# A two-layer encoder on one core: other loads ahead of the weights, x turned through two pairs of banks, and short chains moved between stages

## The chip, the cores and the metric

The kernel runs on one core of a Trainium2 chip. The metric is the device time in microseconds (us), the median of three runs. Lower is better.

## What is computed

Two pre-norm layers over x of 512 tokens by 1024 features, all in float32, with weights read from device memory once. Cut to what matters:

```
# layer 0
h = rmsnorm(x, mix_norm[0]);  proj = h @ w_in             # 1024 x 5376
a_q, a_k = axial_rope(rmsnorm(a_q, q_norm)), axial_rope(rmsnorm(a_k, k_norm))   # 8 / 2 heads of 64
a_o = softmax(a_q * scale @ a_k) @ a_v                    # dense
b_o = mix of three banded attentions (window, dilation) = (128,1), (512,4), (2048,16)
x = x + [a_o, b_o] @ w_out;  x = x + swiglu(rmsnorm(x, ffn_norm[0]))
# layer 1
proj = rmsnorm(x, mix_norm[1]) @ w_in;  u = conv4(proj right) + conv_b
r, i = sigmoid(gate_a(u)), sigmoid(gate_x(u));  log_a = -8 * r * softplus(-lam)
x = x + ((scan forward + scan backward) * gelu(proj left)) @ w_out
x = x + swiglu(rmsnorm(x, ffn_norm[1]));  final rmsnorm
```

## The kernel before, in words

Every product of a weight matrix is made of three TensorE products, high x high, high x low and low x high, written by `mm3` (L1330 to L1332). Activations stand feature by token (`h_hi`, `h_lo`), 8 tiles of 128 features. The weights come in chunks through a ring of four buffers (`RING`). SP loads a chunk into `w_stage` (L360) once the chunk four before it is split (`chunk_lo`). ScalarE copies the high part to `w_hi` (L505) once TensorE has used the chunk four before (`chunk_used`). GpSimd subtracts and writes `w_lo` (L453), and TensorE multiplies. Each engine has its order written out by hand, and semaphores tie them together, so an instruction that waits holds all that is written behind it on its engine.

The order of the stages on TensorE: a prologue; 16 chunks of the first projection (two for each of eight k, 18 products a k); four pairs p = 0 to 3 with 24 chunks each (numbered j = 0 to 23, about nine products each), between whose chunks the attention is woven in; the output projection; the first FFN; the odd layer; the second FFN.

**The prologue.** SP loads x in four parts of 128 tokens (`x_tok`, L371), then the first weight chunks. ScalarE issues 13 small loads (`head_sel`, L556; eight vectors into `p_rows`, L562; the q and k gains into `qk_rows`, L565), then loads its table for the square root (L573) and squares the four parts of x (L578). TensorE turns each part of x (`x_turn`, L1349, eight transposes) into PSUM banks 6 and 7, and VectorE copies them to `x_t` (L863); a turn waits for the copy of the one before. Between turns 1 and 2 TensorE turns the parameter rows (L1365, L1366), once all 13 loads are in. `idle_products` (L1341) are products of zeros whose result nobody reads. After the last copy come the root means: `diag`, a product that spreads them (L1355), `rstd_a`, and h, which is x times gain times root mean.

**The first pair (p = 0).** `first_pair(j)` on TensorE, ScalarE and VectorE holds what turns the first projection into q and k of the dense attention: gains, squares (`sq_qk`), sums of squares by head (L1402, 20 small products, 40 in the trace, with 2 columns each), roots, `k_rb` (L1408), `ak`. The scores of the four blocks (L1430) stand at j = 10, 13, 16 and 19, and the turning of their probabilities (L1442) at j = 13, 16, 19 and 22. VectorE makes the maxima (`a_stat`, L1019), and after ScalarE's exponential (L662) scales the probabilities (`prob_a`, L1027). At j = 11 VectorE also works through `softplus_out` (L925 to L939), 16 instructions of 128x16 that are needed first in the odd layer.

In the first FFN VectorE ends the norm with `rstd_wide` (L968); then come the gate products of a group (L1167), four chunks ahead of which ScalarE and GpSimd must have the next weights split.

## Time and profile before

| | us |
|---|---|
| median of three runs (1390.64 to 1395.12) | 1392.08 |
| the profiled execution, its time | 1390.08 |
| its span | 1388.3 |
| TensorE busy | 1310.5 (94%) |
| GpSimd, VectorE, ScalarE busy | 646.1, 554.7, 549.5 |

The page follows one execution. TensorE is busy for 94% of the span, each other engine for less than half. The chain of work that ended last, by engine: TensorE 51%, issue 21%, GpSimd 11%, VectorE 11%. A view in order of time gives for each merged group its start, its length, the engine, line, operation and operands, and in brackets the idle time before it with what ended it.

### The profile page before, as it was taken

The numbers are of one execution on the slowest core, as the hardware profiler recorded it, in microseconds if no ns is written. First come the engines' busy times: TensorE is split into PE (matmuls) and PEld (weight loads), VectorE is DVE, ScalarE is ACT, GpSimd is POOL, SyncE is SP. The second block draws the span as 40 slices with busy tenths as digits, with TensorE's granted clock in tenths as the row PEclk, the third lists the DMA queues.
The fourth block names the chain that finished last, engine by engine and source line by source line (L and its number), as shares of the span: only waits on it lengthen the run. The fifth ranks groups of instructions, "written<-read, shape, count | busy, mean of one in ns | idle before, by whom it ended". The sixth has DMA issues, their size and how long they took to land.

```text
span 1388.3 us, 18821 instructions
## 1 busy us (share of the span) xinstructions
PE 1310.5 (94%) x6606; PEld 1056.2 (76%) x6606; DVE 554.7 (40%) x881; ACT 549.5 (40%) x999; POOL 646.1 (47%) x512
## 2 busy tenths in 40 slices
PE   7998999999999999999999987957899999999996
PEld 5876787777778888888888876746688888888885
DVE  4358575665644312212102146978652221210102
ACT  3434444444444333333323327558343332332322
POOL 2556464555535444454444443524544444444440
PEclk9999999999999999999999998979899999999997
DMA  4622212222313333333222241213233333332221
GB/s 141 199 57 60 62 55 65 58 66 64 122 52 114 95 96 97 98 97 96 96 97 98 76 148 64 84 47 121 70 105 99 97 92 98 97 100 97 92 91 60
DMA packets 118725, 125.74 MB, mean 91 GB/s; under 512 B 7945, under 2 KB 98313, under 8 KB 118025
## 3 DMA queue, kind: packets, MB, share of 16 engines
q1 hardware_dynamic: 118272, 124.88, 29.0%
q8 instruction: 37, 0.61, 0.2%
q14 instruction: 24, 0.19, 0.0%
q10 hardware_dynamic: 392, 0.07, 0.0%
HBM read 118.62 MB, written 6.29 MB: 90 GB/s over the span
## 4 chain that ended last, share of the span: by engine, by line
PE 51%; issue 21%; POOL 11%; DVE 11%; ACT 4%; DMA 2%; ACTq 0%; POOLq 0%; DVEq 0%; SPq 0%
PE ps L1330 15%; PE ps L1331 14%; PE ps L1332 14%; POOL w_lo L453 10%; DVE r_g L1283 2%; DVE i_g L1278 1%; PE ps L1453 1%; DVE u_f L1214 1%; PE ps L1488 1%; PE ps L1465 1%; PE ps L1430 1%; PE ps L1469 1%; POOL rot L462 1%; DMA w_stage<-in_odd_w_in_dram 1%; DVE a_g L1293 1%
## 5 line engine op out<-in xcount | busy, mean ns | idle before, releaser
L453 POOL TENSOR_TENSOR w_lo<-w_stage,w_hi 128x512 fp32r<-128x512 f32 (+2 forms) x456 | 581.0, 1280 | 711.9 <-ACT w_hi L505 711.7
L505 ACT ACTIVATE w_hi<-w_stage 128x512 fp32r<-128x512 f32 (+2 forms) x456 | 268.8, 595 | 636.9 <-PE ps L1332 622.5
L1330 PE MATMUL ps<-h_hi,w_hi 128*128 128x512 f32 x1104 | 439.6, 398 | 6.3 <-POOL w_lo L453 3.2
L1331 PE MATMUL ps<-h_lo,w_hi 128*128 128x512 f32 x1104 | 431.9, 391 | 0.0
L1332 PE MATMUL ps<-h_hi,w_lo 128*128 128x512 f32 x1104 | 431.7, 391 | 0.0
L1330 PEld LDWEIGHTS ps<-h_hi,w_hi 128*128 128x128 f32 x1104 | 208.8, 189 | 68.0 <-issue 16.5
L1332 PEld LDWEIGHTS ps<-h_hi,w_lo 128*128 128x128 f32 x1104 | 208.4, 189 | 44.1
L1331 PEld LDWEIGHTS ps<-h_lo,w_hi 128*128 128x128 f32 x1104 | 208.9, 189 | 41.9 <-issue 1.0
L1167 DVE TENSOR_TENSOR silu_g<-ps,rstd_wide 128x512 f32<-128x512 f32 x44 | 30.2, 686 | 331.7 <-PE ps L1332 331.7
L1330 PE MATMUL ps<-f_hi,w_hi 128*128 (+1 forms) x352 | 137.0, 389 | 0.0
L1332 PE MATMUL ps<-f_hi,w_lo 128*128 (+1 forms) x352 | 136.9, 389 | 0.0
L1331 PE MATMUL ps<-f_lo,w_hi 128*128 (+1 forms) x352 | 136.9, 389 | 0.0
L1140 DVE TENSOR_TENSOR x_t<-x_t,ps 128x512 f32<-128x512 f32 x32 | 21.0, 681 | 234.6 <-PE ps L1332 234.6
L1330 PEld LDWEIGHTS ps<-f_hi,w_hi 128*128 128x128 f32 x352 | 66.1, 188 | 13.8
L1332 PEld LDWEIGHTS ps<-f_hi,w_lo 128*128 128x128 f32 x352 | 66.1, 188 | 13.7
L1331 PEld LDWEIGHTS ps<-f_lo,w_hi 128*128 128x128 f32 x352 | 66.1, 188 | 13.6
L662 ACT ACTIVATE prob_a<-ps,a_stat,exp_scale 128x512 f32<-128x512 f32 x32 | 24.6, 774 | 52.9 <-DVE a_stat L1020 52.9
L1330 PE MATMUL ps<-s_hi,w_hi 128*128 128x512 f32 x64 | 27.3, 426 | 11.8 <-DVE s_lo L1301 6.0
L1330 PE MATMUL ps<-u_hi,w_hi 128*128 128x512 f32 x32 | 15.7, 492 | 23.5 <-DVE u_raw L1229 16.0
L1332 PE MATMUL ps<-w_hi,h_lo 128*128 128x256 f32 x128 | 36.1, 282 | 0.0
L1330 PE MATMUL ps<-w_hi,h_hi 128*128 128x256 f32 x128 | 36.1, 282 | 0.0
L1331 PE MATMUL ps<-w_lo,h_hi 128*128 128x256 f32 x128 | 36.1, 282 | 0.0
(205 smaller groups left out, 1460.4 us busy)
## 6 DMA issues: line engine op xcount, KB each, us to landing
w_stage<-in_ffn_w_gate_up_dram SPq DMA_DIRECT2D x176, 256.0 KB, 3.1
w_stage<-in_ffn_w_down_dram SPq DMA_DIRECT2D x88, 256.0 KB, 2.7
w_stage<-in_even_w_in_dram SPq DMA_DIRECT2D x96, 192.0 KB, 2.5
w_stage<-in_odd_w_in_dram SPq DMA_DIRECT2D x32, 256.0 KB, 2.5
x_spill<-x_t SPq DMA_DIRECT2D x2, 2048.0 KB, 8.1
x_t<-x_spill SPq DMA_DIRECT2D x2, 2048.0 KB, 7.7
w_stage<-in_odd_w_out_dram SPq DMA_DIRECT2D x16, 256.0 KB, 2.8
w_stage<-in_even_w_out_dram SPq DMA_DIRECT2D x16, 192.0 KB, 2.4
```

Of the source, the lines that this page charges most:

```text
L453: pool.tensor_tensor(out=w_lo[:, s, 0:n], in0=stage[:, s, 0:n], in1=w_hi[:, s, 0:n].bitcast(f32), op=ALU.subtract).then_inc(chunk_lo, 1)
L462: pool.tensor_tensor(out=rot[:, g, :], in0=q_f[:, g, :], in1=tab(K_SINB, T), op=ALU.mult).then_inc(sin_done, 1)
L505: act.activation(w_hi[:, j % RING, 0:n], stage[:, j % RING, 0:n], ACT.Copy).then_inc(chunk_hi, 1)
L662: act.activation(prob_a[:, hh, :], ps[:, hh, :], ACT.Exp, scale=exp_scale[:, p, c, hh:hh + 1], bias=a_stat[:, 1, hh:hh + 1], accum_out=a_s ...
L1140: V.tensor_tensor(x_t[:, j, :], x_t[:, j, :], ps[:, b0 + m, :], ALU.add).then_inc(x_new, 1)
L1167: V.tensor_tensor(silu_g[:, q, :], ps[:, b0 + q, :], rstd_wide[:, :], ALU.mult).then_inc(gate_scaled, 1)
L1214: ins = V.scalar_tensor_tensor(out=u_f[:, n, :], in0=u_raw[:, n % 4, w:w + T], scalar=tap, in1=u_f[:, n, :], op0=ALU.mult, op1=ALU.add)
L1278: driven[t] = step.mark(V.tensor_tensor(i_g[:, t, :], i_g[:, t, :], m_g[:, t, :], ALU.mult))
L1283: scanned[u] = step.mark(V.tensor_tensor_scan(out=r_g[:, u, way], data0=a_g[:, u, way], data1=i_g[:, u, way], initial=0.0, op0=ALU.mult, o ...
L1330: pe.matmul(out_, lh, rh, start=start, stop=False, skip_group_check=skip)
L1331: pe.matmul(out_, lh, rl, start=False, stop=False, skip_group_check=skip)
L1332: return pe.matmul(out_, ll, rh, start=False, stop=stop, skip_group_check=skip)
```

## The change

It does five things.

1. ScalarE issues one load (`mix_norm`, into `mix_rows`) in place of 13. The other 12 are issued by SP, behind the load of weight chunk 4. Those rows are turned on TensorE after k = 5 of the first projection, and copied by VectorE at the end of its first-norm work; the first pair waits for them (`params_ready`).
2. x is turned through banks 6, 7 and 2, 3 by turns, so that a turn waits for the copy of the turn before the last. Fewer idle products stand between.
3. The sums of squares of q and k stand at j = 2, 3, 4 and 5 (4, 4, 8, 4 products) in place of all 20 at j = 4. The turning of v goes from j = 3 to 5, the root from 5 to 6, `k_rb` from 7 to 8, `ak` from 8, 9 to 9, 11.
4. VectorE's `aq_rope(0)` goes from j = 6 to j = 4.
5. `softplus_out` goes from j = 11 of the first pair to the first FFN, behind `rstd_wide`.

```diff
@@ -373,6 +374,17 @@
                 k = c // 2
                 col, n = (512, 256) if c % 2 else (0, 512)
                 load(c, c, stage[:, c % RING, 0:n], w_even[rows(k), col:col + n])
+                if c == 4:
+                    sync.dma_start(head_sel[:, :], A["consts"][:, K_HEAD:K_HEAD + 2]).then_inc(params_in, 16)
+                    for at_, name, n in ((G_FFN, "ffn_norm", 16), (G_FINAL, "final_norm", 8),
+                                         (CONV_W, "odd_conv_w", 32), (CONV_B, "odd_conv_b", 8), (GA_B, "odd_gate_a_b", 16),
+                                         (GX_B, "odd_gate_x_b", 16), (LAM, "odd_lambda", 16)):
+                        v = A[name]
+                        flat = {1: "(n p) -> n p", 2: "l (n p) -> (l n) p", 3: "a l (n p) -> (a l n) p"}[len(v.shape)]
+                        sync.dma_start(p_rows[at_:at_ + n, :], v.rearrange(flat, p=P)).then_inc(params_in, 16)
+                    for n, name in enumerate(("even_q_norm", "even_k_norm")):
+                        for half in range(2):
+                            sync.dma_start(qk_rows[n:n + 1, half * HD:(half + 1) * HD], A[name]).then_inc(params_in, 16)
...
@@ -444,6 +456,7 @@
             pool.memset(ones[:, :], 1.0).then_inc(ones_set, 1)
+            pool.memset(p_rows[0:G_FFN, :], 0.0).then_inc(ones_set, 1)
             pool.memset(bkf[:, :], 0.0).then_inc(pads_zeroed, 1)
@@ -553,16 +566,7 @@
-            act.dma_start(head_sel[:, :], A["consts"][:, K_HEAD:K_HEAD + 2]).then_inc(params_in, 16)
-            for at_, name, n in ((G_MIX, "mix_norm", 16), (G_FFN, "ffn_norm", 16), (G_FINAL, "final_norm", 8),
-                                 (CONV_W, "odd_conv_w", 32), (CONV_B, "odd_conv_b", 8), (GA_B, "odd_gate_a_b", 16),
-                                 (GX_B, "odd_gate_x_b", 16), (LAM, "odd_lambda", 16)):
-                v = A[name]
-                flat = {1: "(n p) -> n p", 2: "l (n p) -> (l n) p", 3: "a l (n p) -> (a l n) p"}[len(v.shape)]
-                act.dma_start(p_rows[at_:at_ + n, :], v.rearrange(flat, p=P)).then_inc(params_in, 16)
...
+            act.dma_start(mix_rows[0:G_FFN, :], A["mix_norm"].rearrange("l (n p) -> (l n) p", p=P)).then_inc(mix_in, 16)
 
             def first_root(c0, c1):
 
@@ -608,18 +613,18 @@
                     for m in (2 * j - 2, 2 * j - 1):
                         act.wait_ge(aq_scaled, m + 1)
                         act.activation(sq_qk[:, m, :], ps[:, m, :], ACT.Square).then_inc(sq_done, 1)
-                if j == 4:
+                if j == 5:
                     act.wait_ge(v_a_turned, 1)
                     act.activation(av[:, :, :].rearrange("p c d -> p (c d)"), ps[:, 2, :], ACT.Copy).then_inc(av_in, 1)
-                if j == 5:
+                if j == 6:
                     act.wait_ge(qk_ms, 1)
                     act.activation(rstd_qk[:, :, :, :], rstd_qk[:, :, :, :], ACT.Sqrt).then_inc(qk_sqrt, 1)
                     act.activation(scratch[:, :], ones[:, 0:1], ACT.Exp)
-                if j == 6:
+                if j == 7:
                     act.wait_ge(lam_exp_in, 1)
                     act.activation(sp[:, 1, :], sp[:, 1, :], ACT.Exp, scale=-1.0).then_inc(lam_exp, 1)
-                if j in (8, 9):
-                    m = j - 8
+                if j in (9, 11):
+                    m = (j - 9) // 2
                     act.wait_ge(k_roped, 1)
                     for half in (m, 1 - m):
                 dve.wait_ge(x_turned, c + 1)
-                V.tensor_copy(x_t[:, :, c * P:(c + 1) * P], ps[:, 6:8, :].rearrange("p b (j t) -> p (b j) t", t=P)).then_inc(x_raw, 1)
+                b0 = 2 if c % 2 else 6
+                V.tensor_copy(x_t[:, :, c * P:(c + 1) * P], ps[:, b0:b0 + 2, :].rearrange("p b (j t) -> p (b j) t", t=P)).then_inc(x_raw, 1)
 
             def first_ms_part(c0, c1):
@@ -890,9 +896,8 @@
-            dve.wait_ge(params_turned, 1)
-            step.mark(V.tensor_copy(params[:, :], ps[:, 1, 0:P]))
-            V.tensor_copy(qk_gain[:, :], ps[:, 1, P:P + 2]).then_inc(params_ready, 1)
+            dve.wait_ge(mix_turned, 1)
+            mix_copied = step.mark(V.tensor_copy(params[:, 0:G_FFN], ps[:, 1, 0:G_FFN]))
             x_in_place(2)
             first_ms_part(0, 3)
@@ -911,6 +916,9 @@
                 h_scaled(k)
             h_lo_part(KD - 2)
             h_lo_part(KD - 1)
+            dve.wait_ge(params_turned, 1)
+            step.mark(V.tensor_copy(params[:, G_FFN:P], ps[:, 6, G_FFN:P]))
+            V.tensor_copy(qk_gain[:, :], ps[:, 6, P:P + 2]).then_inc(params_ready, 1)
 
             def softplus_in():
                     dve.wait_ge(chunk_used, C_PAIR)
@@ -993,10 +1002,13 @@
                 if j == 4:
+                    dve.wait_ge(aq_scaled, 4)
+                    aq_rope(0)
+                if j == 5:
                     dve.wait_ge(ssq_ready, 1)
                     flat = rstd_qk[:, :, :, :].rearrange("p t c h -> p (t c h)")
                     V.tensor_scalar(flat, ps[:, 4, 0:40], 1.0 / HD, EPS, ALU.mult, ALU.add).then_inc(qk_ms, 1)
-                if j == 5:
+                if j == 6:
                     dve.wait_ge(qk_sqrt, 1)
                     flat = rstd_qk[:, :, :, :].rearrange("p t c h -> p (t c h)")
                     step.done(V.reciprocal(flat, flat))
@@ -1004,14 +1016,9 @@
-                if j == 6:
-                    dve.wait_ge(aq_scaled, 4)
-                    aq_rope(0)
-                if j == 7:
+                if j == 8:
                     dve.wait_ge(k_rb, 1)
                     V.tensor_tensor(k_f[:, :], k_f[:, :], ps[:, 3, :], ALU.mult).then_inc(k_roped, 1)
-                if j == 11:
-                    softplus_out()
 
             def a_step(p, c):
@@ -1156,6 +1163,8 @@
 
             def ffn(n, nn, next_gain, fb):
                 late_rms(nn, 4 - fb)
+                if n == 0:
+                    softplus_out()
@@ -1343,10 +1352,11 @@
             def x_turn(c):
 
                 pe.wait_ge(x_in[c], 16)
-                if c:
-                    pe.wait_ge(x_raw, c)
+                if c >= 2:
+                    pe.wait_ge(x_raw, c - 1)
+                b0 = 2 if c % 2 else 6
                 for j in range(KD):
-                    last = pe.transpose(ps[:, 6 + j // 4, (j % 4) * P:(j % 4 + 1) * P], x_tok[:, c, j * P:(j + 1) * P], ident[:, :])
+                    last = pe.transpose(ps[:, b0 + j // 4, (j % 4) * P:(j % 4 + 1) * P], x_tok[:, c, j * P:(j + 1) * P], ident[:, :])
                 last.then_inc(x_turned, 1)
@@ -1359,21 +1369,20 @@
             idle_products(6)
             pe.wait_ge(consts_in, 16)
             x_turn(0)
+            idle_products(2)
+            x_turn(1)
+            pe.wait_ge(mix_in, 16)
+            pe.transpose(ps[:, 1, 0:G_FFN], mix_rows[0:G_FFN, :], ident[0:G_FFN, 0:G_FFN]).then_inc(mix_turned, 1)
+            idle_products(2)
+            x_turn(2)
+            idle_products(2)
+            x_turn(3)
             idle_products(3)
-            x_turn(1)
-            pe.wait_ge(params_in, 16 * 13)
-            pe.transpose(ps[:, 1, 0:P], p_rows[:, :], ident[:, :])
-            pe.transpose(ps[:, 1, P:P + 2], qk_rows[0:2, :], ident[0:2, 0:2]).then_inc(params_turned, 1)
+            pe.wait_ge(ones_set, 2)
+            first_spread(0, 3)
             idle_products(3)
-            x_turn(2)
-            idle_products(4)
-            x_turn(3)
-            idle_products(2)
-            pe.wait_ge(ones_set, 1)
-            first_spread(0, 3)
-            idle_products(4)
             first_spread(3, 4)
-            idle_products(8)
+            idle_products(6)
 
             for k in range(KD):
@@ -1384,24 +1393,29 @@
+                if k == 5:
+                    pe.wait_ge(params_in, 16 * 12)
+                    pe.transpose(ps[:, 6, 0:P], p_rows[:, :], ident[:, :])
+                    pe.transpose(ps[:, 6, P:P + 2], qk_rows[0:2, :], ident[0:2, 0:2]).then_inc(params_turned, 1)
 
 
             def first_pair(j):
 
-                if j == 3:
+                if j in (2, 3, 4, 5):
+                    for t in {2: (4,), 3: (0,), 4: (1, 2), 5: (3,)}[j]:
+                        pe.wait_ge(sq_done, 1 if t == 4 else t + 2)
+                        for c in range(NC):
+                            at_ = 2 * (NC * t + c)
+                            last = pe.matmul(ps[:, 4, at_:at_ + 2], sq_qk[:, t, c * P:(c + 1) * P], head_sel[:, :], start=True, stop=True)
+                    if j == 5:
+                        last.then_inc(ssq_ready, 1)
+                if j == 5:
                     pe.wait_ge(v_f_in, 1)
-                    pe.wait_ge(sq_done, 5)
                     pe.wait_ge(aq_scaled, 4)
                     for c in range(NC):
                         last = pe.transpose(ps[:, 2, c * P:(c + 1) * P], v_f[:, c * P:(c + 1) * P], ident[:, :])
                     last.then_inc(v_a_turned, 1)
-                if j == 4:
-                    for t in range(5):
-                        for c in range(NC):
-                            at_ = 2 * (NC * t + c)
-                            last = pe.matmul(ps[:, 4, at_:at_ + 2], sq_qk[:, t, c * P:(c + 1) * P], head_sel[:, :], start=True, stop=True)
-                    last.then_inc(ssq_ready, 1)
-                if j == 7:
+                if j == 8:
                     pe.wait_ge(half_ones_set, 3)
                     pe.wait_ge(k_diag, 2)
@@ -1542,6 +1556,8 @@
                     attention(p, j)
                     c = C_PAIR + p * PAIR_CHUNKS + j
                     part, k = divmod(j, KD)
+                    if p == 0 and j == 0:
+                        pe.wait_ge(params_ready, 1)
                     chunk_ready(c)
                     s = c % RING
                     if part < 2:
```

On TensorE in the prologue the program has these rows. `zeros` are the idle products, `ident,x_tok` a turn of x, `diag,ones` the spreading of the root means. Before:

```order
L1341 MATMUL ps<-zeros 128x512 x6
L1349 MATMUL ps<-ident,x_tok 128x128 x8
L1341 MATMUL ps<-zeros 128x512 x3
L1349 MATMUL ps<-ident,x_tok 128x128 x8
L1365 MATMUL ps<-ident,p_rows 128x128
L1366 MATMUL ps<-ident,qk_rows 128x2
L1341 MATMUL ps<-zeros 128x512 x3
L1349 MATMUL ps<-ident,x_tok 128x128 x8
L1341 MATMUL ps<-zeros 128x512 x4
L1349 MATMUL ps<-ident,x_tok 128x128 x8
L1341 MATMUL ps<-zeros 128x512 x2
L1355 MATMUL ps<-diag,ones 128x384
```

The same place after the change:

```order
L1350 MATMUL ps<-zeros 128x512 x6
L1359 MATMUL ps<-ident,x_tok 128x128 x8
L1350 MATMUL ps<-zeros 128x512 x2
L1359 MATMUL ps<-ident,x_tok 128x128 x8
L1375 MATMUL ps<-ident,mix_rows 128x16
L1350 MATMUL ps<-zeros 128x512 x2
L1359 MATMUL ps<-ident,x_tok 128x128 x8
L1350 MATMUL ps<-zeros 128x512 x2
L1359 MATMUL ps<-ident,x_tok 128x128 x8
L1350 MATMUL ps<-zeros 128x512 x3
L1365 MATMUL ps<-diag,ones 128x384
```

Behind turn 1 stands one turn of `mix_rows` where the two turns of all parameters stood.

On VectorE at j = 10 to 13 of the first pair, before (`a_stat` and `prob_a` belong to the dense attention, `softplus_work` to the odd layer, `rot` and `bq` to the rotary part of the banded one):

```order
L1025 RECIPROCAL a_stat<-a_stat 128x2
L1027 TENSOR_SCALAR prob_a<-prob_a,a_stat 128x512 x2
L925 TENSOR_SCALAR softplus_work<-softplus_work 128x16
L926 RECIPROCAL softplus_work<-softplus_work 128x16
L927 TENSOR_TENSOR softplus_work<-softplus_work 128x16
...
L939 TENSOR_SCALAR decay_neg<-softplus_work 128x16
L1055 STREAM_SHUFFLE rot<-rot 128x512
L1066 TENSOR_TENSOR bq<-q_f,rot 128x4x4x32
L1078 COPY pta<-ps 128x4x128
L1019 TENSOR_REDUCE a_stat<-ps 128x2
```

And after:

```order
L1032 RECIPROCAL a_stat<-a_stat 128x2
L1034 TENSOR_SCALAR prob_a<-prob_a,a_stat 128x512 x2
L1062 STREAM_SHUFFLE rot<-rot 128x512
L1073 TENSOR_TENSOR bq<-q_f,rot 128x4x4x32
L1085 COPY pta<-ps 128x4x128
L1026 TENSOR_REDUCE a_stat<-ps 128x2
```

The softplus rows are gone from between `prob_a` and the next maximum; they now stand between `rstd_wide` and the first gate product of the first FFN.

## Rows read from the trace of the kernel before

**Rows 1.** Timeline of PE, prologue: start us, us, engine, line, op, operands, [idle<-releaser]

```profile
6.11 1.06 PE L1349 MATMUL ps<-ident,x_tok 128*128 128x128 f32 x8 [1.86 <-DMA x_tok<-in_x_dram]
...
11.61 0.38 PE L1365 MATMUL ps<-ident,p_rows 128*128 128x128 f32 x1 [1.97 <-DMA qk_rows<-in_even_k_norm_dram]
...
13.56 1.82 PE L1349 MATMUL ps<-ident,x_tok 128*128 128x128 f32 x8
...
26.18 0.50 PE L1330 MATMUL ps<-h_hi,w_hi 128*128 128x512 f32 x1 [0.71 <-DVE h_lo L889]
```

**Rows 2.** Timeline of DVE, prologue

```profile
7.21 1.23 DVE L863 COPY x_t<-ps 128x1024 f32<-128x1024 f32 x1 [5.80 <-PE ps L1349]
...
17.90 1.22 DVE L863 COPY x_t<-ps 128x1024 f32<-128x1024 f32 x1 [1.18 <-PE ps L1349]
```

**Rows 3.** Timeline of ACT, prologue

```profile
7.11 1.28 ACT L573 ACT_TABLE_LOAD   x1 [7.11 <-issue]
```

**Rows 4.** The tile `x_tok`: time from issue to landing of its four loads

```profile
DMA to landing us min/median/max: 4.8/6.1/7.7
```

**Rows 5.** Timeline of SP, the loads of x and of chunks 4 and 5

```profile
1.20 1.85 SPq L371 DMA_DIRECT2D x_tok<-in_x_dram  x4
...
19.89 2.16 SPq L360 DMA_DIRECT2D w_stage<-in_even_w_in_dram  x2
```

**Rows 6.** DMA issues of the first 60 us: count, KB each, median us to landing

```profile
w_stage<-in_even_w_in_dram SPq DMA_DIRECT2D x8, 256.0 KB, 2.8
```

**Rows 7.** Windows: us, PE, PEld, DVE, ACT, POOL busy (count), granted clock, DMA, GB/s

```profile
19.00:20.00 1.00, 0.00 (x0) 0.00 (x0) 0.97 (x3) 0.00 (x0) 0.86 (x1) 1.00 0.00 0
...
73.00:75.00 2.00, 2.00 (x7) 1.57 (x6) 0.00 (x0) 0.00 (x0) 0.00 (x0) 0.55 0.00 0
75.00:77.00 2.00, 2.00 (x7) 1.54 (x7) 0.06 (x1) 0.72 (x3) 0.14 (x1) 0.60 0.00 0
...
110.00:115.00 5.00, 4.56 (x16) 2.38 (x17) 4.96 (x6) 2.45 (x5) 4.96 (x4) 0.66 0.36 103
```

**Rows 8.** Timeline of PE, first pair, from the sums of squares to j = 19

```profile
68.16 4.52 PE L1402 MATMUL ps<-head_sel,sq_qk 128*128 128x2 f32 x40
...
80.37 1.88 PE L1408 MATMUL ps<-diag,half_ones 128*128 128x512 f32 x4
...
85.59 0.47 PE L1330 MATMUL ps<-h_hi,w_hi 128*128 128x512 f32 x1 [1.25 <-ACT q_f L634]
...
97.20 1.03 PE L1442 MATMUL ps<-ident,prob_a 128*128 128x128 f32 x8
...
110.02 0.63 PE L1442 MATMUL ps<-ident,prob_a 128*128 128x128 f32 x4 [4.38 <-DVE prob_a L1027]
...
120.69 0.63 PE L1442 MATMUL ps<-ident,prob_a 128*128 128x128 f32 x4
```

**Rows 9.** Timeline of PE, second pair, j = 13 and j = 19

```profile
181.08 1.03 PE L1442 MATMUL ps<-ident,prob_a 128*128 128x128 f32 x8
...
197.94 0.63 PE L1442 MATMUL ps<-ident,prob_a 128*128 128x128 f32 x4
```

**Rows 10.** Timeline of DVE, first pair, j = 11

```profile
96.55 1.26 DVE L925 TENSOR_SCALAR softplus_work<-softplus_work 128x16 f32<-128x16 f32 x1
...
103.51 0.17 DVE L935 TENSOR_SCALAR softplus_work<-softplus_work 128x16 f32<-128x16 f32 x1
...
104.14 0.17 DVE L939 TENSOR_SCALAR decay_neg<-softplus_work 128x16 f32<-128x16 f32 x1
```

**Rows 11.** Timeline of DVE, then of ACT, start of the first FFN

```profile
451.43 0.69 DVE L968 COPY rstd_wide<-ps 128x512 f32<-128x512 f32 x1 [4.02 <-PE ps L1595]
454.27 0.69 DVE L1167 TENSOR_TENSOR silu_g<-ps,rstd_wide 128x512 f32<-128x512 f32 x1 [2.15 <-PE ps L1332]
...
458.73 0.61 ACT L505 ACTIVATE w_hi<-w_stage 128x512 fp32r<-128x512 f32 x1
```

**Rows 12.** Timeline of POOL, first pair, j = 11

```profile
96.31 1.47 POOL L468 TENSOR_TENSOR q_f<-q_f,table 128x512 f32<-128x512 f32 x1
```

12 lines of the change are left out of this document (6 added, 6 removed).

## The prediction, made before the changed kernel ran
> **What bounds the kernel now.** I read the shares of busy time first: TensorE works 94% of the span, so what counts is where it waits and where its clock is low. The list of its waits and the windows with the granted clock then show three places that this change touches. (1) The prologue. The first product of the first projection starts at 26.18 us [rows 1]. TensorE had turned parts 0 and 1 of x by 9.64 us, then sat 1.97 us until the last of ScalarE's 13 small loads was in, at 11.61, and turn 2, at 13.56, took 1.82 us for what turn 0 did in 1.06 [rows 1]. The copy of part 3 starts on VectorE at 17.90 [rows 2], and from there a chain of copies, root means and h runs to 26.18. (2) The middle of the first pair. Forty products of two columns keep TensorE busy for 4.52 us [rows 8]; just behind them the clock is 0.55 and 0.60 for 4 us, half speed (1.2 in place of 2.4 GHz) for most of it [rows 7]. A wait of 1.25 us for ScalarE's `q_f` follows at j = 8 [rows 8]. (3) The turn at j = 16, which waits 4.38 us for `prob_a` [rows 8], with the clock at 0.66 over the 5 us from 110 [rows 7]. VectorE was at `softplus_out` from 96.55 to 104.31 us, 7.8 us in all [rows 10], and its next maximum stands behind that. From the projection at 26.18 up to the sums TensorE has no gap to speak of: 8 x 18 + 4 x 9 = 180 products from 26.18 to 68.16, less some 0.6 us for turning v, is 0.23 us each; so a k takes 4.1 us and a chunk of the pair 2.1.
>
> **The prologue.** With one load on its queue instead of 13, ScalarE's table load (at 7.11 [rows 3]) and its squares no longer come behind the issues; the squares then follow the landing of x. The loads of x land 4.8 to 7.7 us after issue [rows 4]; the last of the four goes out at about 2.6 [rows 5], so it is in by 10.3. Turn 0 is bound by its load, as before: 6.11 to 7.17, copy 7.21 to 8.44 [rows 1, 2]. Turn 1 goes to the other banks: two idle products (0.5, estimated from 0.23 each) put it at 7.7 to 8.8, copy to 10.05. The turn of `mix_rows` and its copy of 16 columns are an estimate of 0.2 us each. Turn 2 runs from 9.6 to 10.7, copy 10.75 to 12.0, two idle products, turn 3 from 11.2 to 12.3 (its load is in), copy 3 at 12.35. Against 17.90 this is 5.5 us earlier, and all behind it (first mean, `diag`, spreading, h) is the same chain of the same lengths. It also needs ScalarE's square of part 3, which as before fits beside copy 3. I take **5.5**. Floor: if the clock is low in the turns as it was in turn 2, two turns cost 0.76 more each, so 4.0. Ceiling: part 3 in at 10.3 and turned at once gives a copy at 11.4, 6.5.
>
> **The 12 loads on SP.** They stand behind the load of chunk 4, issued at 19.89 before [rows 5], so at about 14.4. At the pace of ScalarE's queue (13 issues before 7.11 [rows 3], so at most 0.55 each) they take 6.6 us; chunk 5 goes out at 21.4 and lands 2.8 later [rows 6], at 24.2. SP's own pace was 1.85 for four [rows 5], 0.46. ScalarE can't split it before TensorE has used chunk 1, at 20.7 + 4.1 = 24.8, and TensorE wants it at 20.7 + 8.2 + 12 x 0.23 = 31.7, less some 1.5 for split and subtraction: it must be in by 30.2, 6.0 us later than it is. That cover makes the issues **0**, and it lasts until each issue takes 0.55 + 6.0/12 = 1.05 us. The two transposes of these rows, put between chunks of a full TensorE, cost what they cost: the first was 0.38 [rows 1], so **-0.5** for both, between 0 and -0.8. `params_ready` is set near 20.7 + 6 x 4.1 = 45.3, and asked for at 53.5.
>
> **Sums of squares.** The 20 products cost the same in total. Split 4, 4, 8, 4 with a full chunk between, the longest run is 1.8 us instead of 4.5. An empty TensorE for 1.0 us of [rows 7] (19 to 20), in a gap of 2.1 us, left the clock at 1.00, while 4.5 us of two-column products did not; 1.8 us is nearer to the first. So I let the low clock go: 2 x 0.45 + 2 x 0.40 = **1.7** us back [rows 7]. It can be 0 too. Three more switches between small and large products cost an estimated one small product each (4.52 / 40 = 0.11), **-0.3**, at most -0.6.
> The Trainium skill (TensorE: Matmul & The Clock Gate, HAM oscillation) puts the fall of the clock down to idle stretches between groups of matmuls. By that rule a TensorE that is busy throughout 68 to 73 us should not slow, and spreading would give nothing: the sum would be 1.7 less. The trace speaks against the rule read so narrowly, since the fall follows 4.52 us without a gap [rows 7, 8]; the rule is kept as the first rival.
>
> **j = 8.** `k_rb` took up to 1.88 us of TensorE at j = 7 [rows 8]. At j = 8 it stands where TensorE waited 1.25 us for the copy of `q_f`, and needs none of the copied banks. So the wait goes: **+1.25** (at least 0.4). What is late next is `ak`: the copies now stand at j = 9 on ScalarE behind the split of a chunk, and end about when TensorE reaches the scores at j = 10. I put **-0.2** for it, between 0 and -0.5. `aq_rope(0)` at j = 4 fills idle time of VectorE; the root, at j = 6, leaves over 1 us before `k_rb` needs `diag`.
>
> **softplus away from j = 11.** The same stretch, j = 13 to j = 19, is 197.94 - 181.08 = 16.86 us in the second pair [rows 9] and 120.69 - 97.20 = 23.49 in the first [rows 8]. Both hold the same chunks, turns and scores; the difference of **6.6** is the wait of 4.38 and the clock that fell after it (5 x 0.34 = 1.7 [rows 7]), with 0.5 of other. Without softplus VectorE gets to rotary work at 96.6, waits for GpSimd's 1.47 us [rows 12] until 97.8, and finds the scores done near 99.3 (the turn at 97.20 takes 1.03 [rows 8], four score products an estimated 0.27 each). The maximum over 1024 columns costs about what a copy of as many does, 1.23 [rows 2], with a small step behind it, so 100.8. Two exponentials on ScalarE and two scalings, each of 512 columns at an estimated 0.8 (0.69 for such a copy [rows 11]), with the handing over, end near 104.5. TensorE was at j = 16 at 110.02 - 4.38 = 105.64 [rows 8]. There is 1 us to spare. I allow 5.5 to 7.
>
> **softplus in the FFN.** VectorE is idle from 452.12 to 454.27 there [rows 11]. The 16 instructions take 0.21 us each when nothing disturbs them (103.51 to 104.14 is three steps [rows 10]), 3.4 in all, and 7.8 as measured at j = 11. So the gate products come 1.3 to 5.6 us late, and ScalarE, which stands behind them, makes its next split at 458.73 [rows 11] plus that. TensorE asks for that chunk four chunks (4 x 12 x 0.23 = 11.0) after 454.2, at 465.2, and split (0.61) and subtraction (an estimated 1.5, by the 1.47 of [rows 12]) take 2.1: 465.2 - 2.1 - 458.7, up to 4.4 us of delay are free. I take **0**, since GpSimd has only one or two subtractions in that stretch, and 5.6 - 4.4 = 1.2 lost as the floor.
> The Trainium skill (SBUF — State Buffer, two separate sides) says that VectorE and GpSimd share a port pair which one holds for a whole instruction. The trace agrees: 128x16 took 1.26 us beside GpSimd at 96.55 and 0.17 at 103.51 [rows 10]. By it two holds of 1.5 us make 3.4 + 3.0 - 2.1, a delay of 4.3: still free, but barely, which is why the rival below keeps a chance.
>
> **Sum.** 5.5 - 0.5 + 1.7 - 0.3 + 1.25 - 0.2 + 6.6 = 14.0 us. The profiled execution took 1390.1 (span 1388.3, 1.8 around it), so 1376.1; the median is 2.0 above it, so **1378.0**. No later stage is changed but the FFN.
>
> **Rivals.**
> - The low clock stays with the small products, or comes elsewhere in the pair: 1.7 less, 1379.8. For it: all 4.5 us of them still lie within four chunks. Against: full chunks between them.
> - The clock falls at the start of the projection, since only six idle products stand ahead of it and TensorE's gap of about 2 us before the spreading is still there. The first 3 us at half speed cost 1.7, with one slow turn 2.5: 1380.5.
> - The turn at j = 16 still waits, because VectorE's rotary additions wait for GpSimd one by one (1.47 us each [rows 12]). Half of the 6.6 would then stay: 1381.3. That this part of the change does nothing at all would be 1384.6.
> - softplus starves the ring in the FFN: 1.2, so 1379.2.
> - Slower: the 12 small loads hold up the weight loads on SP's queue. From 1.05 us an issue on, TensorE waits for chunk 5, and each further 0.1 us costs 1.2. All of the gain is gone at 1.05 + 14.0/12 = 2.2 us; at 2.6 the time is 1396.7. For it: no row shows twelve small loads in a row on this queue, behind and ahead of large ones. Against: 0.46 to 0.55 an issue in the rows there are.
>
> **How the numbers follow.** Forecast 0.60, clock in the pair 0.15, clock at the start 0.10, turn at j = 16 0.07 (of which 0.02 for no effect), FFN 0.05, SP's queue 0.03. The bounds added up give a gain between 4.0 - 0.8 + 0 - 0.6 + 0.4 - 0.5 + 5.5 - 1.2 = 6.8 and 6.5 + 0 + 1.7 + 0 + 1.25 + 0 + 7 = 16.5; it is unlikely that all are at one end. I take 8.5 to 16.5 off the median of 1392.1, and below that the 1.4 us by which the fastest run of before lies under its median: 1374.0 to 1383.5. A difference of 0.3% (4.2 us) is about what a measurement can tell from none. Faster by more than that: 0.95; within it 0.03; slower 0.02 (SP's queue, from 2.6 us an issue on).
>
> **What would show it.** In the profile of the changed kernel: first product of the projection at 20 to 21.5 us; no wait of TensorE for `qk_rows`; SP's 12 issues within 6 us and no wait of TensorE for `w_lo` near 31; clock 1.00 through j = 2 to 8; no wait for `q_f` at j = 8; j = 13 to 19 in about 17 us; softplus at the first FFN in 3.4 to 6 us, with no wait of TensorE for `w_lo` behind it. I am wrong above all if the projection does not start 5 us earlier, or if the two places of low clock only move.

## The result, and the profile after

| | before | after |
|---|---|---|
| median of the runs on the same chip, us | 1392.24 (1390.64 to 1395.12, 4 runs) | 1378.47 (1378.13 to 1379.78, 4 runs) |
| ratio, with its 95% interval | | 0.9901 (0.9883 to 0.9918) |
| profiled execution: time, span | 1390.08, 1388.3 | 1378.48, 1376.7 |
| TensorE busy | 1310.5 | 1307.0 |

The changed kernel is 13.8 us faster; 1378.0 was forecast, with a range of 1374.0 to 1383.5. Its page shows where TensorE's clock is still low: the row of the granted clock in 40 slices of the span.

```profile
PEclk9999999999999999999999989978999999999997
```

No slice of the first 23 is low. What is left lies at the end of the first FFN and in the odd layer (from about 804 us), and at the very end. The row can't show what the change did, since none of the first 24 slices is low before either: a few us at half clock disappear in a slice of 35. (In the rows, PE is TensorE, PEld its weight loads, DVE VectorE, ACT ScalarE, POOL GpSimd, and SPq the queue that SP issues loads on.) The prologue after, on TensorE, to be held against [rows 1] (start, length, engine, line, operation, operands, idle time before and its releaser):

```profile
5.62 1.06 PE L1359 MATMUL ps<-ident,x_tok 128*128 128x128 f32 x8 [1.38 <-DMA x_tok<-in_x_dram]
...
7.23 1.09 PE L1359 MATMUL ps<-ident,x_tok 128*128 128x128 f32 x8
8.25 0.23 PE L1375 MATMUL ps<-ident,mix_rows 16*128 16x16 f32 x1
...
18.48 0.50 PE L1339 MATMUL ps<-h_hi,w_hi 128*128 128x512 f32 x1 [1.20 <-DVE h_lo L895]
```

On VectorE, against [rows 2]:

```profile
11.39 1.22 DVE L869 COPY x_t<-ps 128x1024 f32<-128x1024 f32 x1
...
12.73 0.56 DVE L862 TENSOR_TENSOR diag<-ident,rstd 128x384 f32<-128x384 f32 x1
```

The projection starts at 18.48 us, 7.70 earlier than in [rows 1]. The first pair on TensorE, against [rows 8]:

```profile
61.88 1.84 PE L1409 MATMUL ps<-head_sel,sq_qk 128*128 128x2 f32 x16
...
79.11 1.13 PE L1444 MATMUL ps<-ak,aq_f 64*128 64x512 f32 x4
86.45 1.03 PE L1456 MATMUL ps<-ident,prob_a 128*128 128x128 f32 x8
...
94.73 1.04 PE L1456 MATMUL ps<-ident,prob_a 128*128 128x128 f32 x8
...
103.83 0.63 PE L1456 MATMUL ps<-ident,prob_a 128*128 128x128 f32 x4 [0.44 <-DVE prob_a L1034]
```

The turn at j = 16 waits for nothing. Starts of the same instruction in both profiled executions give the account of the whole (the lead is before minus after):

| start of | before | after | lead |
|---|---|---|---|
| the first projection | 26.18 | 18.48 | 7.70 |
| scores at j = 10 | 89.86 | 79.11 | 10.75 |
| turn at j = 13 | 97.20 | 86.45 | 10.75 |
| turn at j = 16 | 110.02 | 94.73 | 15.29 |
| turn at j = 19 | 120.69 | 103.83 | 16.86 |
| `rstd_wide` of the first FFN | 451.43 | 436.11 | 15.32 |
| `rstd_wide` of the odd layer | 818.52 | 803.89 | 14.63 |
| `rstd_wide` of the second FFN | 1027.26 | 1015.65 | 11.61 |
| the end of the span | 1388.3 | 1376.7 | 11.6 |

So 16.9 us are won by j = 19, and 5.3 are gone again by the second FFN: 1.5 up to the first FFN, 0.7 in it and 3.0 in the odd layer. Of these stages the change touches only the first FFN. That is what the experiments had to explain, beside the size of each part.

### The profile page after: what moved, and what is told of

It reads as the page before. It is cut to its first block, busy times and chain, and to the rows that moved or that the text cites. A ratio compares the mean times of both kernels' runs of the same rounds, so it can differ in the third digit from the quotient of the medians.

```text
span 1376.7 us, 18816 instructions
## 1 busy us (share of the span) xinstructions
PE 1307.0 (95%) x6601; PEld 1054.1 (77%) x6601; DVE 552.9 (40%) x882; ACT 549.5 (40%) x999; POOL 641.0 (47%) x513
## 4 chain that ended last, share of the span: by engine, by line
PE 55%; issue 19%; POOL 10%; DVE 10%; ACT 4%; DMA 1%; POOLq 0%; DVEq 0%; SPq 0%; ACTq 0%
PE ps L1339 16%; PE ps L1341 16%; PE ps L1340 16%; POOL w_lo L466 9%; DVE r_g L1292 2%; DVE i_g L1287 1%; PE ps L1467 1%; PE ps L1502 1%; PE ps L1479 1%; PE ps L1483 1%; PE ps L1444 1%; POOL rot L475 1%; DVE a_g L1302 1%; DVE r_g L1271 1%; ACT a_g L807 1%
## 5 line engine op out<-in xcount | busy, mean ns | idle before, releaser
L466 POOL TENSOR_TENSOR w_lo<-w_stage,w_hi 128x512 fp32r<-128x512 f32 (+2 forms) x456 | 574.8, 1266 | 705.3 <-ACT w_hi L518 705.2
L1340 PEld LDWEIGHTS ps<-f_lo,w_hi 128*128 128x128 f32 x352 | 66.1, 188 | 13.8
```

The lines of the kernel that those rows point to most:

```text
L466: pool.tensor_tensor(out=w_lo[:, s, 0:n], in0=stage[:, s, 0:n], in1=w_hi[:, s, 0:n].bitcast(f32), op=ALU.subtract).then_inc(chunk_lo, 1)
L1340: pe.matmul(out_, lh, rl, start=False, stop=False, skip_group_check=skip)
```

## The experiments

Each kernel is the changed one with one edit, unless it says otherwise. Kernels of one group ran on one chip beside the same runs of the kernel before. With the median stand the lowest and highest run and their count. Where a median is said to be so much more, it is against the changed kernel's 1378.47, taken in the first comparison, or 1378.58 (a_same, third group); the first group has no run of the changed kernel on its own chip.

### First group: each part undone

The kernel before took 1391.7 here (1388.61 to 1396.14, 17 runs).

**a_soft**: softplus back at j = 11.

```diff
@@ VectorE, first_pair
+                if j == 11:
+                    softplus_out()
@@ VectorE, ffn
-                if n == 0:
-                    softplus_out()
```

> The changed kernel with softplus_out put back at j = 11 of the first pair. Term for softplus: TensorE's stretch from j = 13 to j = 19 goes from 17.4 us back to about 23.5, with a wait of about 4.4 us at the turn of j = 16 and a low clock behind it; the time rises by 5 to 7 us, to about 1384.5. Rival (the turn at j = 16 was late for another reason, VectorE's rotary additions behind GpSimd): the stretch stays within 1 us of 17.4 and the time within 1.5 us. The FFN should not move by more than 0.3 us by either.

Measured: 1385.04 (1382.02 to 1386.71, 6), ratio 0.9944 (0.992 to 0.9967): 6.6 more than the changed kernel's 1378.47. Its rows at j = 13 and 16 on TensorE:

```profile
87.93 1.03 PE L1456 MATMUL ps<-ident,prob_a 128*128 128x128 f32 x8
...
100.71 0.78 PE L1456 MATMUL ps<-ident,prob_a 128*128 128x128 f32 x4 [4.34 <-DVE prob_a L1036]
```

and on VectorE, the first softplus instruction and the maximum that stands behind the last:

```profile
87.28 1.25 DVE L933 TENSOR_SCALAR softplus_work<-softplus_work 128x16 f32<-128x16 f32 x1
...
96.77 1.21 DVE L1028 TENSOR_REDUCE a_stat<-ps 128x2 f32<-128x1024 f32 x1
```

In the changed kernel this maximum starts 2.62 us behind the turn at j = 13, here 8.84:

```profile
89.07 1.21 DVE L1026 TENSOR_REDUCE a_stat<-ps 128x2 f32<-128x1024 f32 x1
```

The wait of 4.38 in [rows 8] is back as 4.34, and j = 13 to 19 takes 23.46 us (before 23.49, after 17.38).

**b_soft**: the kernel before, with only this edit of the change made.

```diff
@@ VectorE, first_pair
-                if j == 11:
-                    softplus_out()
@@ VectorE, ffn
+                if n == 0:
+                    softplus_out()
```

> The kernel before with one edit, softplus_out moved to the first FFN. My term gives 6.6 us less (5.5 to 7): about 1385.5 on a median of 1392.2, with the wait for prob_a at j = 16 gone and the stretch from j = 13 to j = 19 at about 17 us. Rival (the gain needs the other parts, since q_f or ak would be late next): less than 3 us.

Measured: 1387.67 (1383.92 to 1388.61, 10), ratio 0.9963 (0.9948 to 0.9978), 4.0 less than before. In its trace j = 13 to 19 takes 17.36 us, 6.1 less. From both sides the trace gives 6.1; the two medians, 6.6 and 4.0, lie about it, and the interval of the second (3.1 to 7.2 us) holds it. By the median alone the expectation of 5.5 to 7 was missed, and 4.0 is above the rival's 3 as well: it is the trace that decides. This kernel has the prologue of before, and its projection starts at 24.55, not at the 26.18 of [rows 1]:

```profile
24.55 0.50 PE L1330 MATMUL ps<-h_hi,w_hi 128*128 128x512 f32 x1 [0.16 <-DVE h_lo L889]
```

So the old prologue too has no fixed length.

**a_sums4**: all sums of squares at j = 4 again.

```diff
-                if j in (2, 3, 4, 5):
-                    for t in {2: (4,), 3: (0,), 4: (1, 2), 5: (3,)}[j]:
+                if j == 4:
+                    for t in (4, 0, 1, 2, 3):
```

> The changed kernel with all 20 products of the sums of squares at j = 4 again, all else as changed. My term: behind 4.5 us of two-column products the granted clock falls to half for about 3.4 us, and the first pair is 1.7 us longer less 0.3 for three switches, so the scores at j = 10 start 1.4 us later. Rival (the clock falls only behind idle stretches): clock 1.00 from j = 2 to j = 8, the scores at j = 10 within 0.4 us of where they were, or earlier by 0.3. In the time either may be hidden by where the clock falls later (up to 2 us).

Measured: 1382.19 (1381.91 to 1383.64, 5), ratio 0.9931 (0.9905 to 0.9957), 3.7 more. Two of its windows (length, then busy time and count of PE, PEld, DVE, ACT, POOL; the third figure from the end is the granted clock), and its sums:

```profile
66.00:68.00 2.00, 2.00 (x11) 2.00 (x11) 0.00 (x0) 0.00 (x0) 0.00 (x0) 0.50 0.00 0
68.00:70.00 2.00, 2.00 (x6) 1.61 (x6) 0.20 (x1) 0.00 (x0) 0.00 (x0) 0.50 0.00 0
```
```profile
61.46 6.57 PE L1409 MATMUL ps<-head_sel,sq_qk 128*128 128x2 f32 x40
```

TensorE is busy for the whole of both windows, at half its clock; the clock is 0.90 in the window from 62 us, 0.50 in the four from 64 and 1.00 again from 74. The stretch from projection to scores takes 65.44 us where the changed kernel takes 60.63. The price of the bunch here, 4.8 us by the trace, is well over the 1.4 that was expected and the 1.7 that [rows 7] gave: the clock fell while the sums still ran, so that they too were slow. It is also more than the change can have gained by it, since the whole stretch got only 3.05 shorter.

**a_bank1**: all four turns of x through banks 6 and 7.

```diff
 VectorE:
-                b0 = 2 if c % 2 else 6
+                b0 = 6
 TensorE:
-                if c >= 2:
-                    pe.wait_ge(x_raw, c - 1)
-                b0 = 2 if c % 2 else 6
+                if c:
+                    pe.wait_ge(x_raw, c)
+                b0 = 6
```

> The changed kernel with x turned through banks 6 and 7 alone, so that each turn waits for the copy before it. If the banks are what brought the copies together: turns start 1.2 us after each copy began, copy 3 starts at about 14 us in place of 11.4 and the projection at about 21 in place of 18.5, so 2.5 us more. If the loads alone did it: the projection within 0.7 us of 18.5.

Measured: 1381.74 (1381.07 to 1382.45, 5), ratio 0.992 (0.9895 to 0.9944), 3.3 more. Each turn now waits for the copy of the one before:

```profile
5.79 1.94 PE L1359 MATMUL ps<-ident,x_tok 128*128 128x128 f32 x8 [1.54 <-DMA x_tok<-in_x_dram]
...
14.14 1.06 PE L1359 MATMUL ps<-ident,x_tok 128*128 128x128 f32 x8 [0.94 <-DVE x_t L869]
...
23.51 0.50 PE L1339 MATMUL ps<-h_hi,w_hi 128*128 128x512 f32 x1 [1.17 <-DVE h_lo L895]
```

The other kernels with the new prologue start their projection between 19.5 and 20.7 (the first profile of after alone at 18.48). So of what the prologue gained, the second pair of banks carries 2.8 to 5.0, and the median says 3.3. Not all of it is the turns: copy 3 starts at 15.24, and behind it the two `diag` instructions take 1.04 and 1.06 us as in before, where the other kernels with the new prologue have 0.56 and 0.32. That is 1.2 of the difference.

### Second group: the small loads, `k_rb`, and what a later start costs

The kernel before took 1394.11 here (1389.82 to 1395.71, 8 runs).

**a_krb7**: `k_rb` and what VectorE does with it back at j = 7.

```diff
@@ VectorE, first_pair, and the same on TensorE
-                if j == 8:
+                if j == 7:
```

> The changed kernel with k_rb and its use on VectorE back at j = 7. My term: TensorE waits 1.25 us for q_f at j = 8 again, so the scores at j = 10 start about 1.2 us later than the 79.11 us of the changed kernel and the time rises by 1.2. Rival (the products of k_rb only moved the wait): a new wait for diag at j = 7 or none at all, and less than 0.4 us of difference.

Measured: 1379.27 (1378.22 to 1380.63, 4), ratio 0.9903 (0.9876 to 0.993). Its waits there:

```profile
74.36 1.96 PE L1422 MATMUL ps<-diag,half_ones 128*128 128x512 f32 x4 [0.97 <-DVE diag L862]
...
79.65 0.47 PE L1339 MATMUL ps<-h_hi,w_hi 128*128 128x512 f32 x1 [1.25 <-ACT q_f L639]
```

The 1.25 of [rows 8] is back, to the hundredth, and since the root now stands at j = 6 a wait of 0.97 for `diag` comes with it. Projection to scores takes 63.35 us, 2.7 more, where 1.2 was expected. Yet the median is only 0.7 above a_same, the changed kernel in the next group; see there.

**a_act12**: the 12 small loads on ScalarE's queue again, behind `mix_norm`.

```diff
@@ SP
-                if c == 4:
-                    sync.dma_start(head_sel[:, :], A["consts"][:, K_HEAD:K_HEAD + 2]).then_inc(params_in, 16)
...
@@ ScalarE, behind the load of mix_rows
+            act.dma_start(head_sel[:, :], A["consts"][:, K_HEAD:K_HEAD + 2]).then_inc(params_in, 16)
...
```

> The changed kernel with the 12 small loads back on ScalarE's queue behind mix_norm's, nothing on SP's. If the issues on ScalarE held up the squares: table load at about 7 us instead of 1.2, squares from 8.4, the third ready at about 12 in place of 9.6, and the projection starts 0.5 to 2 us later than 18.48. If they did not matter once TensorE no longer waits for the last landing: within 0.4 us. Landing of x 0.5 us later (4.8 in place of 4.3 us for the first) if the small packets compete with it.

Measured: 1379.19 (1378.17 to 1380.23, 4), ratio 0.9902 (0.9875 to 0.9928). The table load is late again, as in [rows 3], and the first part of x came late, with a slow turn behind it:

```profile
7.02 1.28 ACT L576 ACT_TABLE_LOAD   x1 [7.02 <-issue]
```
```profile
6.37 1.94 PE L1358 MATMUL ps<-ident,x_tok 128*128 128x128 f32 x8 [2.13 <-DMA x_tok<-in_x_dram]
...
21.62 0.50 PE L1338 MATMUL ps<-h_hi,w_hi 128*128 128x512 f32 x1 [1.21 <-DVE h_lo L894]
```

The projection starts at 21.62, 3.1 us later than in the first profile of the changed kernel and 1.0 to 2.1 later than in the others with the loads on SP. The late squares of ScalarE are not the reason: from copy 3 (14.54) to the projection it takes 7.08 us, and 7.09 in after. The time went in the turns, the first two of which took 1.94 and 1.91. Nor is a late landing of x shown to come from the small loads, since in a_sums4z, with them on SP, the first turn starts as late (6.39). The medians (1379.19 against 1378.47 and 1378.58) can't be told apart.

**a_sp36**: 36 more small loads on SP between chunks 4 and 5, into rows that nobody reads.

```diff
+                    for r in range(36):
+                        sync.dma_start(qk_rows[32 + r:33 + r, 0:HD], A["even_q_norm"]).then_inc(params_in, 16)
...
-                    pe.wait_ge(params_in, 16 * 12)
+                    pe.wait_ge(params_in, 16 * 48)
```

> The changed kernel with 36 more small loads (one row of 64 numbers each, 0.28 us an issue in the rows) behind chunk 4's on SP's queue, 10 us more. They write rows that nothing uses. The cover of the prediction, with the 4.5 us that the 12 issues took: chunk 5 may be 5.6 us later before TensorE waits for it. So TensorE waits about 4.5 us for w_lo near 29 us, and the time rises by 4 to 5.5 us. Rival (the ring gives no such cover, a late chunk is felt at once): 9 to 10 us. Other rival (SP's queue has more cover, or small loads overlap): under 1.5 us.

Measured: 1385.05 (1382.47 to 1386.27, 5), ratio 0.9936 (0.9914 to 0.9957), 6.6 more. On SP, on ScalarE and on TensorE:

```profile
19.78 10.58 SPq L386 DMA_DIRECT2D qk_rows<-in_even_q_norm_dram  x36
...
31.59 1.30 SPq L361 DMA_DIRECT2D w_stage<-in_even_w_in_dram  x3
```
```profile
33.68 0.42 ACT L520 ACTIVATE w_hi<-w_stage 128x256 fp32r<-128x256 f32 x1 [9.93 <-DMA w_stage<-in_even_w_in_dram]
```
```profile
34.96 0.79 PE L1341 MATMUL ps<-h_hi,w_hi 128*128 128x512 f32 x1 [3.78 <-POOL w_lo L468]
```

The 10.58 us on the queue (0.29 a load) came out as 3.78 of waiting, so the cover left behind the 12 loads is 6.8 us. The product behind the wait takes 0.79 in place of 0.39: the clock had fallen, and is 0.50 from 34 to 40 us. So the wait of 3.78 cost 6.6, by the stretch from projection to scores (67.20 us) as by the median, where 4 to 5.5 was expected. The slower rival's mechanism exists, and the changed kernel keeps well clear of it.

**a_shift**: more idle products ahead of the projection, so that all behind it comes later.

```diff
-            idle_products(6)
+            idle_products(16)
```

> The changed kernel with 16 idle products instead of 6 ahead of the projection, 2.3 us more of which 1.2 fall into a wait: the projection starts 1.1 us later, at 19.6. If the later stages only shift: the span is 1.1 us longer and each later stage keeps its length. If where the clock falls depends on when a wait comes (the lead of the changed kernel was 16.9 us at j = 22 and 11.6 at the end): the first projection to j = 22 keeps its length, but stretches behind 380 us differ by multiples of about 1.7 us either way.

Measured: 1379.17 (1377.81 to 1380.05, 4), ratio 0.9899 (0.9872 to 0.9925). The projection starts at 21.18, 2.7 later than in the first profile of the changed kernel and 0.5 to 1.7 later than in the others with this prologue. The end comes no later that can be told.

### Third group: what lowers the clock, and where it is still to be had

The kernel before took 1393.18 here (1388.47 to 1395.73, 10 runs). **a_same** is the changed kernel, unedited.

> The changed kernel again, unchanged, for the length of its stages in another execution. If the 1.6 us lost near 386 us and the 3.0 us lost in the odd layer were the clock's moment and no effect of the change, the stages from j = 13 to the first rstd_wide and from the second to the third take either of the values seen in the other runs (348.1 or 349.8; 208.8 to 211.8). If they belong to the change they are 349.7 and 211.8 again. Start of the projection between 18.5 and 21 us by the same token, against 18.48 at first.

Measured: 1378.58 (1378.02 to 1379.72, 6), ratio 0.9901 (0.9884 to 0.9919). Its first turn of x:

```profile
5.53 1.94 PE L1359 MATMUL ps<-ident,x_tok 128*128 128x128 f32 x8 [1.28 <-DMA x_tok<-in_x_dram]
```

The same eight turns took 1.94 here and 1.06 in the first profile of this kernel. The wait ahead doesn't decide it: 1.28, 1.54 (a_bank1) and 2.13 (a_act12) went with 1.94, while 1.38, the 1.86 of [rows 1] and 2.14 (a_sums4z) went with 1.06. Its projection starts at 19.52. The two stages asked about take 349.71 and 211.07 us, both long again. By itself this speaks for a loss that belongs to the change; the other runs, taken up at the end of the next section, speak against it for the first stage and leave it open for the second.

**a_sums4z**: the sums at j = 4, with two products of zeros, 512 columns each, ahead of each four.

```diff
-                if j in (2, 3, 4, 5):
-                    for t in {2: (4,), 3: (0,), 4: (1, 2), 5: (3,)}[j]:
+                if j == 4:
+                    pe.wait_ge(sq_done, 5)
+                    pe.wait_ge(aq_scaled, 4)
+                    for t in (4, 0, 1, 2, 3):
+                        for _ in range(2):
+                            pe.matmul(ps[:, 2, :], zeros[:, 0:P], zeros[:, :], start=True, stop=True)
```

> All 20 products of the sums of squares at j = 4, as in the run with all at j = 4 before, but with two products of zeros of 512 columns ahead of each group of four, ten in all or 2.3 us more work. They write a bank that nobody reads then. If the clock fell there because two-column products stream almost nothing, it stays at 1.00 and the scores at j = 10 start 60.6 + 2.3 = 62.9 us behind the start of the projection, 2.5 us less than the 65.4 without the zeros. If the fall has nothing to do with columns (chance, or the moment), the clock falls again and it is 67 us or more.

Measured: 1382.06 (1379.0 to 1384.03, 4), ratio 0.9918 (0.9893 to 0.9942). From the projection to the scores it takes 67.77 us, 2.3 more than in a_sums4, which is just the ten products added. TensorE did not wait, and the clock fell all the same, within the third of five groups (the second and the fourth):

```profile
63.86 0.95 PE L1413 MATMUL ps<-head_sel,sq_qk 128*128 128x2 f32 x8
...
67.41 1.70 PE L1413 MATMUL ps<-head_sel,sq_qk 128*128 128x2 f32 x8
```

So the reading "an unbroken run of small products lowers the clock, and wide ones between them keep it up" fell, at least with two wide ones for each eight small. What holds is narrower: in all four profiled executions with the sums at j = 4 (before, b_soft, a_sums4, a_sums4z) the granted clock falls to 0.50 there, and in all ten with the sums over four chunks it is 1.00 from 54 to 80 us. What it is in the bunch that lowers the clock stays open.

**a_fill**: products of zeros put into TensorE's waits in the output projection, ahead of the odd norm, and in the odd layer. They add zeros to a bank in use, or write one that is free. Beside the table below, 1.6 us of them stand ahead of the last chunks of the output projection and 3.2 us ahead of the sum for the odd norm.

```diff
+            def fill(us, bank, fresh=False):
+                for _ in range(int(us / 0.23)):
+                    pe.matmul(ps[:, bank, :], zero_w[:, :], zero_w[:, :].unsqueeze(1).to_broadcast([P, NC, P]),
+                              start=fresh, stop=fresh, skip_group_check=True)
...
+            FILL = {("i", 0): (1.8, 0, None), ("u1", 0): (3.0, 0, (gelu_in, 4)), ("i", 1): (1.9, 0, None),
+                    ("b1", 0): (1.7, 4, (sig_done, 16)), ("r", 2): (11.6, 4, None), ("i", 2): (1.9, 4, None),
+                    ("o0", 0): (2.7, 4, (gelu_in, 8)), ("o1", 0): (2.7, 4, None), ("o0", 6): (6.0, 4, None)}
```

> The changed kernel with products of zeros in TensorE's waits of the output projection and the odd layer (eleven places, about three quarters or more of each wait, added with no effect to a bank that is being summed or written to a free one). If the low clock behind the waits costs time there (some 12 us of half speed while TensorE works, about 6 to 10 us lost between 386 and 980 us), it gains 3 to 8 us over the changed kernel. If what bounds the odd layer is VectorE's and ScalarE's chain, the higher clock only makes the waits longer: within 1.5 us. If the zeros overrun the waits: slower by up to 3 us.

Measured: 1372.39 (1370.81 to 1373.72, 5), ratio 0.9854 (0.9834 to 0.9875): 6.2 less than a_same on the same chip. TensorE's work got longer by 160 products, and the kernel shorter. The waits tell why (waiting line, releaser, us in all, times, longest). The changed kernel's five longest of the odd layer (first profile):

```profile
PE ps L1339 <- DVE u_raw L1238: 14.4, 2, 12.6
PE ps L1339 <- POOL w_lo L466: 8.7, 3, 3.5
PE ps L1339 <- ACT r_g L783: 7.4, 4, 2.3
PE ps L1339 <- DVE s_lo L1310: 6.6, 1, 6.6
PE ps L1339 <- issue: 3.2, 1, 3.2
```

and a_fill's:

```profile
PE ps L1357 <- DVE gelu_g L1284: 6.5, 2, 3.3
PE ps L1341 <- ACT r_g L785: 4.2, 2, 2.2
PE ps L1341 <- DVE u_raw L1240: 2.6, 2, 1.9
PE ps L1341 <- DVE s_lo L1312: 0.2, 1, 0.2
```

Two fills stood behind the wait for `gelu_g` that they were to cover, and ran on after it. The clearest gain is in the first FFN, at whose end TensorE waits 3.4 us for the sum of squares: behind that wait the clock is 0.50 from 795 to 800 us in a_same and 1.00 in a_fill, and the stage takes 364.8 us, where the twelve kernels without fills have 367.1 to 368.0.

### Fourth: the fills mended

**a_fill2** is a_fill with four fills moved or shortened and one added at the end, beside 1393.53 for the kernel before (1388.43 to 1395.93, 9 runs). The edit is shown against a_fill.

```diff
-            FILL = {("i", 0): (1.8, 0, None), ("u1", 0): (3.0, 0, (gelu_in, 4)), ("i", 1): (1.9, 0, None),
-                    ("b1", 0): (1.7, 4, (sig_done, 16)), ("r", 2): (11.6, 4, None), ("i", 2): (1.9, 4, None),
-                    ("o0", 0): (2.7, 4, (gelu_in, 8)), ("o1", 0): (2.7, 4, None), ("o0", 6): (6.0, 4, None)}
+            FILL = {("i", 0): (3.4, 0, None), ("u1", 0): (1.4, 0, (gelu_in, 1)), ("i", 1): (1.9, 0, None),
+                    ("b1", 0): (1.7, 4, (sig_done, 16)), ("r", 2): (11.6, 4, None), ("i", 2): (3.4, 4, None),
+                    ("o0", 0): (1.4, 4, (gelu_in, 5)), ("o1", 0): (2.7, 4, None), ("o0", 6): (6.0, 4, None)}
...
+            pe.wait_ge(x_new, 3 * KD + 5)
+            fill(5.2, 4, True)
```

> The kernel of a_fill (zero products in TensorE's waits of the output projection and of the odd layer) with its four wrongly placed fills mended and one more at the end. In a_fill the fills ahead of two gate products stood behind the gelu wait and ran 5.88 and 5.06 us at a low clock, longer than the wait they should cover; here they are 1.4 us long and the rest of the wait is filled before it. At the end TensorE waits 6.5 us for y_f and then works 5.6 us at half clock; 5.2 us of zero products stand in that wait. If the clock is what these waits cost: 2 to 5 us less than a_fill's 1372.4, that is 1367.5 to 1370.5. Rival, the chain of VectorE and ScalarE sets the odd layer whatever TensorE's clock is: only the end gains, 1 to 2.5 us, 1370 to 1371.5. Rival, the fills overrun their waits: no less than a_fill, 1372 or more.

Measured: 1369.36 (1369.1 to 1371.01, 5), ratio 0.9831 (0.9812 to 0.9851), the fastest kernel of this study, 24.2 us under the kernel before on the same chip. The page's clock row, to be held against the one at the top:

```profile
PEclk9999999999999999999999999999999999999999
```

The end, from TensorE's last work: the changed kernel, then a_fill2.

```profile
1360.00:1365.00 5.00, 1.08 (x5) 1.11 (x6) 2.81 (x5) 4.57 (x7) 0.00 (x0) 0.50 0.00 0
1365.00:1370.00 5.00, 4.32 (x21) 3.83 (x19) 1.45 (x4) 1.53 (x5) 0.00 (x0) 0.50 0.00 0
```
```profile
1354.79 2.65 PE L1357 MATMUL ps<-zero_w 128*128 128x512 f32 x11
1357.89 1.50 PE L1634 MATMUL ps<-ident,y_f 128*128 128x128 f32 x12 [0.44 <-ACT y_f L547]
```

By stage, in the profiled executions (lengths between the starts of `rstd_wide`, and to the span's end):

| us | first FFN | odd layer | second FFN to end |
|---|---|---|---|
| a_same | 367.43 | 211.07 | 360.5 |
| a_fill | 364.79 | 209.03 | 361.0 |
| a_fill2 | 364.87 | 208.00 | 359.1 |

The end gained 1.9 and the odd layer 1.0; the medians say 3.0, between two groups on two chips. The mean clock of the odd layer is now 0.99, and it takes 208.0 us. The kernel before had 208.74 at a mean clock of 0.89. So a higher clock gains little there; that the chain of the other engines sets the pace is likely, but was not tried.

## Why the prediction held, point by point

- **Prologue: 5.5 predicted. Against the 26.18 of [rows 1] it is 7.7 in the first profile of after, 6.7 in a_same and 5.5 to 6.3 in seven others with the same prologue; against the 24.55 of b_soft it is 1.6 less each time, 3.9 at least.** The mechanism was right, and the term lies within what the executions give. Copy 3 was put at 12.35; it stands at 11.39 in after, 12.44 in a_same and 13.48 in a_krb7. Behind it, `diag` made a difference that was not foreseen: the step "the same chain of the same lengths" failed. Its two instructions took 1.04 and 1.07 us in the trace of before and 0.56 and 0.33 in after; the differences, 0.48 and 0.74, are all that the chain from copy 3 to the projection got shorter (7.09 us, before 8.28). The first met GpSimd before, which was busy for 0.86 of the 1 us from 19 [rows 7], and ends at 13.29 now, as GpSimd starts its first subtraction at 13.23. The second has GpSimd at work on both sides in after too; why it takes 0.33 all the same was not tried. With one pair of banks (a_bank1) both are long. The reason for the low end, slow turns, was real: in a_same the first took 1.94.
- **Transposes of the parameters: -0.5.** They take 0.27 and 0.22 at 43.10. Right.
- **The 12 loads: 0.** SP issues them in 4.5 us, from 14.90 to 19.43, where 6.6 was put, and TensorE waits for no chunk. a_sp36 puts the cover left behind them at 6.8, the prediction at 6.0. With the issues that is 11.3 against 12.6 in all: the cover was overrated by 1.3, the issues by 2.1.
- **Projection to scores: 1.7 - 0.3 + 1.25 - 0.2, with the transposes 1.95 in all; 3.05 measured** (10.75 - 7.70). The clock is 1.00 throughout, the wait for `q_f` at j = 8 is gone, and so is anything for `ak`, for which 0.2 was put. The low clock of before costs 1.7 over 72 to 78 us too, so with 1.25, a wait of 0.23 ahead of the turning of v that is gone as well, and the transposes some 2.7 is accounted for; 0.4 is not. The rival in which the low clock stays had the Trainium skill's rule behind it (TensorE: Matmul & The Clock Gate, HAM oscillation), that idle stretches between groups of matmuls bring the clock down. The trace of before and a_sums4 speak against so narrow a reading: TensorE had no idle time in the windows where the clock fell. Undone alone, the spreading cost 3.7 us and `k_rb` 0.7.
- **softplus away from j = 11: 6.6 predicted, 6.1 measured** (17.38 against 23.49 for j = 13 to 19). The missing 0.5 is, but for 0.1, the wait of 0.44 ahead of the turn at j = 19; the second pair, from which the 6.6 was read, has none there. The predicted timing, scores done near 99.3 and scalings done near 104.5, against a TensorE that comes at 105.64: shifted by the lead of 10.75 it makes 88.6, 93.8 and 94.9. In after the maximum starts at 89.07 and the scalings end at 94.23, 0.5 us ahead of the turn at 94.73. The spare of 1 us was half that, and it was enough.
- **softplus in the FFN: 0, measured 0.** The first FFN takes 367.75 us in a_soft, without softplus in it, and 367.78 in after. It runs from 436.84 to 441.6 (4.7 us; 3.4 to 6 was put), with one instruction of 1.20 beside GpSimd where the same kind takes 0.17. The gate product starts at once behind it:

```profile
439.77 1.20 DVE L943 TENSOR_SCALAR softplus_work<-softplus_work 128x16 f32<-128x16 f32 x1
...
441.51 0.68 DVE L1176 TENSOR_TENSOR silu_g<-ps,rstd_wide 128x512 f32<-128x512 f32 x1
```

- **"No later stage is changed but the FFN": wrong as to time.** 16.9 us were won by j = 19, 11.6 at the end. The total came so close by luck, since three things met: the early stages gave 2.9 more than the sum of 14.0, 5.3 went later, and 2.2 came back because the profiled execution of before lay 2.2 under its median while that of after lies on its own. Where the 5.3 went is measured; what sets it off was found only in part.

The loss has two main places; the 0.7 in the first FFN is not softplus (a_soft has it too), and its cause is open. From the turn at j = 13 to the first `rstd_wide` a kernel with softplus moved takes one of two lengths, whatever its edit: 348.1 us (a_sums4, a_krb7, a_act12, a_shift, a_sums4z, a_fill, a_fill2) or 349.7 to 349.8 (after, a_same, b_soft, a_bank1, a_sp36). The difference arises at one place in the output projection. TensorE waits 1.88 us for `o_lo` in both; what comes behind it, first in after and then in a_shift, is

```profile
385.81 0.50 PE L1339 MATMUL ps<-o_hi,w_hi 128*128 128x512 f32 x1 [1.88 <-DVE o_lo L1096]
...
388.13 0.63 PE L1340 MATMUL ps<-o_lo,w_hi 128*128 128x512 f32 x1
```
```profile
388.43 0.50 PE L1339 MATMUL ps<-o_hi,w_hi 128*128 128x512 f32 x1 [1.88 <-DVE o_lo L1096]
...
390.16 0.39 PE L1340 MATMUL ps<-o_lo,w_hi 128*128 128x512 f32 x1
```

The granted clock is 0.50 from 388 to 390 us in after and 1.00 throughout in a_shift. The kernel before has no low clock at this place either.

The second place is the odd layer, between the second and third `rstd_wide`: 208.74, 208.81 and 208.87 us in before, b_soft and a_krb7, 210.9 to 211.8 in the nine others that have no fills there. a_krb7 has the changed kernel's odd layer and before's length, so that code can run in the short time. Whether the change makes the long one likelier is open: both kernels with the old prologue are short, and one of ten with the rest of the change. It also shows, for the profiled execution, why undoing `k_rb` cost 2.7 us in the pair and little at the end.

Here the clock explains only a part. Its mean over the odd layer is 0.89 in before, b_soft and a_krb7, and 0.89 in a_same and 0.90 in after. a_sums4z (210.94 us) keeps step with before (208.74) for 137.8 us into the layer. Then VectorE rounds into `s_hi`, and GpSimd starts a subtraction 0.04 us behind it, in both. In before VectorE goes first and GpSimd takes long; in a_sums4z VectorE loses 1.1 us, and what TensorE waits for comes so much later. Before, then a_sums4z:

```profile
956.30 0.77 DVE L1298 CAST s_hi<-a_g 128x512 fp32r<-128x512 f32 x2
956.34 5.49 POOL L453 TENSOR_TENSOR w_lo<-w_stage,w_hi 128x512 fp32r<-128x512 f32 x1 [2.48 <-ACT w_hi L505]
```
```profile
948.72 1.85 DVE L1307 CAST s_hi<-a_g 128x512 fp32r<-128x512 f32 x2
948.76 1.53 POOL L466 TENSOR_TENSOR w_lo<-w_stage,w_hi 128x512 fp32r<-128x512 f32 x1 [2.49 <-ACT w_hi L518]
```

The other 1.1 us come behind the wait for `s_lo`, where the clock is low for longer: from there to the next sum into `x_t` it takes 8.35 us, and 7.20 in before.

a_fill bears on this, but less than its short stages suggest. Its 348.1 is the length that five kernels without fills have too, and its 209.0 is no less than the 208.7 of before. What decides, without the fills, whether a given wait is followed by a low clock was not found. It is no matter of the start alone, since a_shift, which starts late, has the short first stretch and the long odd layer.

## What to carry to other kernels

Short work that nobody needs soon does not belong ahead of a maximum that a softmax waits for: seven to eight microseconds of 128x16 instructions in that place cost six on TensorE, and none where VectorE stood idle. Cost each part of a change in the stage where it acts, but expect the total to move by some us from stages that it doesn't touch, where TensorE waits or VectorE and GpSimd meet; compare stage lengths over several profiles before a loss or a gain is put down to an edit. And where TensorE waits for a chain of others, put harmless products into the wait, and ahead of what it waits for: here they were worth 9.2 us (1378.58 in a_same, 1369.36 in a_fill2), more than any single part of the change.

## What the runs showed of the hardware that was not expected

- The clock fell with TensorE busy throughout: forty products of two columns took 4.52 us in before and 6.57 in a_sums4, with the granted clock at 0.50 from 64 to 72 us there, and ten products of 512 columns among them did not keep it up.
- The same wait with the same work on either side (1.88 us for `o_lo`) is followed by a low clock in some executions and not in others. At that place it is worth 1.6 us.
- A 128x16 step on VectorE takes 1.20 or 0.17 us, a `diag` of 128x128 1.07 or 0.33. Two roundings of 128x512 into `s_hi`, with a GpSimd subtraction starting 0.04 us behind them, take 0.77 us and the subtraction 5.49, or 1.85 and 1.53. The Trainium skill (SBUF — State Buffer, two separate sides) has a port pair that VectorE and GpSimd share, held for a whole instruction. The long 128x16 step agrees: it starts at 439.77 and ends with GpSimd's subtraction of 1.29 from 439.65. That step has one tensor input only.
- Issues of small loads on SP took 0.29 us each (36 in 10.58) or 0.38 (12 in 4.5), less than the 0.55 that ScalarE's queue had allowed at most.
